# Hymba layer with 32 experts: fourteen expert blocks of up to 64 tokens run as 64-row blocks, high and low parts side by side, two of their eight gate/up slices as plain f32 products

## The reference, cut to what matters

```python
logits = xf @ w_router + b_router            # 512 tokens, 32 experts
top_v, top_e = lax.top_k(logits, 4)          # 4 experts per token: 2048 rows in all
gates = softmax(top_v)
# for every expert e, over the rows that chose it:
gu = xe @ w_gate_up[e] + b_gate_up[e]        # 1024 -> 2048, gate and up interleaved
gate = minimum(gu[..., 0::2], 7);  up = clip(gu[..., 1::2], -7, 7)
act = (up + 1.0) * (gate * sigmoid(1.702 * gate))
y = act @ w_down[e] + b_down[e]              # 1024 -> 1024
out[row_tok] += y * gate_of_row
```

## Time and profile before

| | us |
|---|---|
| time, median of 3 runs (lowest to highest) | 1488.14 (1487.26 to 1488.17) |
| span of the profiled execution, first to last instruction | 1485.0 |
| PE busy | 1443.0 (97%) |
| DVE busy | 1304.8 (88%) |
| ACT busy | 1017.6 (69%) |

### The profile page before, as it was taken

How to read it: one execution, slowest core, us unless ns; L and a number is a source line. 1 busy time by engine, 2 the same in 40 slices (tenths; PEclk the granted TensorE clock), 3 DMA queues, 4 the chain that set the end, 5 groups by cost and what they waited for, 6 DMA issues and landing times.

```text
span 1485.0 us, 21394 instructions
## 1 busy us (share of the span) xinstructions
PE 1443.0 (97%) x7006; PEld 1173.1 (79%) x7006; DVE 1304.8 (88%) x1230; ACT 1017.6 (69%) x913; POOL 274.3 (18%) x282
## 2 busy tenths in 40 slices
PE   6999999899999999999999999999999999999996
PEld 6877866878888888888888888888888888888883
DVE  7358575899999999999999999999999999999998
ACT  6344345377777777777777777777777777777772
POOL 0000000033222222222222232222222222222210
PEclk9999999899999999999999999999999999999998
DMA  9411130499999999999999999999999999999994
GB/s 349 143 58 57 34 142 15 180 327 391 377 388 375 373 379 374 376 367 372 367 370 375 375 377 365 377 377 378 376 377 377 375 375 375 370 377 362 373 378 178
DMA packets 102334, 472.64 MB, mean 318 GB/s; under 512 B 16499, under 2 KB 16539, under 8 KB 68000
## 3 DMA queue, kind: packets, MB, share of 16 engines
q1 hardware_dynamic: 87632, 451.71, 78.0%
q0 software_dynamic: 14672, 20.53, 3.9%
HBM read 467.70 MB, written 22.02 MB: 330 GB/s over the span
## 4 chain that ended last, share of the span: by engine, by line
PE 92%; DVE 6%; DMA 1%; ACT 1%; issue 1%; SPq 0%; DVEq 0%
PE gu_bank L1321 18%; PE gu_bank L1322 18%; PE gu_bank L1323 18%; PE turn_bank L1321 8%; PE turn_bank L1323 8%; PE turn_bank L1322 8%; PE bank L1608 2%; PE bank L1615 2%; PE bank L1321 1%; PE bank L1323 1%; PE bank L1322 1%; PE gu_bank L1461 1%; PE gu_bank L1601 1%; DMA arena<-in_x_dram 1%; DVE w_lo L873 1%; PE turn_bank L1487 1%
## 5 line engine op out<-in xcount | busy, mean ns | idle before, releaser
L873 DVE TENSOR_TENSOR w_lo<-raw,w_hi 128x2048 fp32r<-128x2048 f32 x411 | 931.7, 2289 | 98.3 <-ACT w_hi L605 93.5
L605 ACT ACTIVATE w_hi<-raw 128x2048 fp32r<-128x2048 f32 x411 | 784.6, 1920 | 209.1 <-PE gu_bank L1323 176.0
L1321 PE MATMUL gu_bank<-w_hi,turned 128*128 128x512 f32 x1080 | 423.8, 392 | 1.2 <-ACT arena L795 1.1
L1323 PE MATMUL gu_bank<-w_hi,turned 128*128 128x512 f32 x1080 | 420.5, 389 | 0.0
L1322 PE MATMUL gu_bank<-w_lo,turned 128*128 128x512 f32 x1080 | 420.4, 389 | 0.0
L1321 PEld LDWEIGHTS gu_bank<-w_hi,turned 128*128 128x128 f32 x1080 | 202.8, 188 | 43.6 <-ACT arena L795 1.4
L1323 PEld LDWEIGHTS gu_bank<-w_hi,turned 128*128 128x128 f32 x1080 | 202.7, 188 | 42.3
L1322 PEld LDWEIGHTS gu_bank<-w_lo,turned 128*128 128x128 f32 x1080 | 202.9, 188 | 40.7
L1321 PE MATMUL turn_bank<-w_hi,turned 128*128 128x512 f32 (+1 forms) x544 | 213.4, 392 | 0.0
L1323 PE MATMUL turn_bank<-w_hi,turned 128*128 128x512 f32 (+1 forms) x544 | 210.4, 387 | 0.0
L1322 PE MATMUL turn_bank<-w_lo,turned 128*128 128x512 f32 (+1 forms) x544 | 210.3, 387 | 0.0
(11 more groups left out here) (297 smaller groups left out, 1352.3 us busy)
## 6 DMA issues: line engine op xcount, KB each, us to landing
raw<-in_w_gate_up_dram SPq DMA_DIRECT2D x264, 1024.0 KB, 8.1
raw<-in_w_down_dram SPq DMA_DIRECT2D x132, 1024.0 KB, 8.9
raw<-in_w_in_dram SPq DMA_DIRECT2D x10, 1024.0 KB, 6.8
raw<-in_w_out_dram SPq DMA_DIRECT2D x4, 1024.0 KB, 5.0
raw<-expert_rows SPq DMA_DIRECT2D x4, 1024.0 KB, 6.4
raw<-in_w_mem_kv_dram SPq DMA_DIRECT2D x2, 1024.0 KB, 12.1
arena<-in_x_dram SPq DMA_DIRECT2D x1, 2048.0 KB, 13.7
arena<-in_position_tables_dram SPq DMA_DIRECT2D x1, 2048.0 KB, 18.0
```

Of the source, the lines that this page charges most:

```text
L605: a.activation(home, raw_ap, ACT.Copy).then_inc(hi_ready, 1)
L873: v.tensor_tensor(home[1], raw_ap, home[0].bitcast(F32), ALU.subtract).then_inc(lo_ready, 1)
L1321: pe.matmul(bank, a[0], b[0], start=first, stop=False)
L1323: return pe.matmul(bank, a[1], b[0], start=False, stop=last)
```

## The change

The changed kernel has two kinds of block. Fourteen experts of at most 64 tokens each (of the experts 1 to 31, in their order) become the odd blocks 1, 3, ..., 27: *narrow* blocks. All other blocks are *wide*, as before. Steps 1 to 28 thus form 14 pairs; step `b` with odd `b` does the gate/up of a narrow block and the down of a wide one (called here a narrow step), the next does the gate/up of a wide and the down of a narrow block (a wide step).

- In a narrow block `hx` holds the high parts of 64 rows in columns 0 to 63 and their low parts in columns 64 to 127, and `ha` likewise. A product is two matmuls (`two`: both halves times `w_hi`, both times `w_lo`), eight a slice; output rows 64 to 127 then hold what the low parts gave and are added to rows 0 to 63 later, by matmuls with a shifted identity (`fold_gate_up`, 4 matmuls, after d0; `fold_down`, 2 matmuls, after k0 of the next step), each behind a copy of the bank by ACT (`low_of_gate_up`, 128 x 2048; `low_of_down`, 128 x 1024).
- Slices k1 and k5 of a narrow block are not split. SP loads them into one buffer, `spare`; PE multiplies them as f32, four matmuls of 128 x 512 (`gate_up_whole`). The slot of `raw` and the counts of `lo_ready` that they would have had are stepped over.
- The clamp of a narrow block waits for its fold (`gu_folded`), and works on 64 rows. The rows of a narrow block leave one step later (`y_out_folded`), and POOL's scatter is one step later for every block. The loads of `g_final` and the down biases move behind the pairs.
- The routing finds the narrow experts and numbers the blocks anew: three small DVE instructions go and some twenty come.

The core of the diff (declarations, tables and the other engines' calls left out):

```diff
+            def whole(e, j, b):
+
+                k = WHOLE[j]
+                sp.wait_ge(lo_ready, b * 12 + (7 + k))
+                sp.sem_inc(raw_in[(GU + k) % 6], 16)
+                sp.wait_ge(half_used, b * 12 + (9 + k))
+                sp.dma_start(spare.rearrange("p (e n) -> p e n", e=1),
+                             gu_dram[bass.ds(e, 1), :, k, :].rearrange("e p n -> p e n")).then_inc(whole_in[j], 16)
...
+            def narrow_step(b):
+
+                before, e = experts_of(b)
+                for k in range(GU):
+                    if k == WHOLE[1]:
+                        whole(e, 0, b)
+                    elif k != WHOLE[0]:
+                        gate_up(e, k, GU + k, b * 12 + (7 + k))
+                for j in range(DN):
+                    if j == 2:
+                        whole(e, 1, b)
+                    down(before, j, 2 * GU + j, b * 12 + (7 + GU + j))
+
+            with sp.Fori(0, NARROW) as n:
+                narrow_step(n * 2 + 1)
+                wide_step(n * 2 + 2)
+            with sp.Fori(LOOP_FROM - 1, loops + 1) as b:
+                wide_step(b)
...
+            def narrow_after_wide(b, folded):
+
+                hi_m(GU + 4, b, 2)
+                if folded is not None:
+                    y_out_folded(folded, column(b - 2), b * 16)
+                hi_m(GU + 6, b)
+                turn_act(0, b)
+                turn_act(1, b)
+                for i in range(7, 11):
+                    hi_m(GU + i, b)
+                low_of_gate_up(b + 1)
+                hi_m(GU + 11, b)
...
-            link(v.tensor_scalar(n_blk, count, float(P), 1.0, ALU.is_gt, ALU.add))
-            for j in (2, 3):
-                link(v.scalar_tensor_tensor(out=n_blk, in0=count, scalar=float(P * j), in1=n_blk,
-                                            op0=ALU.is_gt, op1=ALU.add))
+            link(v.scalar_tensor_tensor(out=few, in0=count, scalar=NARROW_ROWS + 0.5, in1=cst[:, C_NOT_FIRST:C_NOT_FIRST + E],
+                                        op0=ALU.is_lt, op1=ALU.mult))
+            link(v.tensor_tensor_scan(few_seen, ones[:, 0:E], few, 0.0, ALU.mult, ALU.add))
...
+            def wide_after_narrow(b, narrow_next):
+
+                for i in range(4, 7):
+                    lo_m(GU + i, b)
+                turn_act_narrow(0, b * 2)
+                turn_act_narrow(1, b * 2 + 1)
+                for i in range(7, 11):
+                    lo_m(GU + i, b)
+                clamp(b + 1)
+                lo_m(GU + 11, b)
+                for q in range(2):
+                    if narrow_next:
+                        turn_x_narrow(q, b * 2 + (3 + q))
+                    else:
+                        turn_x(q, b * 2 + (3 + q))
+                activate(b + 1, b)
+                lo_m(GU + 12, b, 2 if narrow_next else 1)
+                for i in range(14 if narrow_next else 13, 16):
+                    lo_m(GU + i, b)
...
+            def two(bank, a, b, first=False, last=False):
+
+                pe.matmul(bank, a, b[0], start=first, stop=False)
+                return pe.matmul(bank, a, b[1], start=False, stop=last)
...
+            def gate_up_whole(j, n):
+
+                k = WHOLE[j]
+                pe.wait_ge(whole_in[j], n * 16)
+                for c in range(4):
+                    ins = pe.matmul(psum[c], hx[:, k, :].bitcast(F32), spare[:, c * 512:(c + 1) * 512],
+                                    start=False, stop=False)
                 ins.then_inc(half_used, 1)
...
+            def narrow_after_wide(b, n, between=None):
+
+                pe.wait_ge(xlo_ready, b * 2 + 2)
+                for k in range(GU):
+                    if k in WHOLE:
+                        gate_up_whole(WHOLE.index(k), n)
+                    else:
+                        gate_up(k, GU + k, b, between=between if k == 0 else None, narrow=True)
+                    if k == 0 and between is None:
+                        fold_down(n - 1)
+                    if k == 2:
+                        turn_acts(b)
+                gu_bias(b, narrow=True)
+                pe.wait_ge(alo_ready, b * 2)
+                turn_rows(b * 16 + 16)
+                pe.wait_ge(y_free, b)
+                for j in range(DN):
+                    down(j, 2 * GU + j, b)
+                    if j == 0:
+                        fold_gate_up(n)
```

More of the change, by code:

```diff
@@ L212, in hymba_layer @@
         n_blk = small(E)
+        few_seen, narrow_index, narrow_rows = (small(E) for _ in range(3))
+        rows_i = small(E).bitcast(I32)
+        narrow_from = small(E)
+        blk_two = small(NT * TOPK)
+        exp_wide, few = F[:, 15144:15144 + MAX_BLOCKS], F[:, 15192:15192 + E]
         b_end = small(E)
@@ L251, in hymba_layer @@
         g_final = F[:, 11264:12288]
+        spare = F[:, 11264:13312]
         back = raw[:, 0:NT, :]
@@ L581, in _, with steps @@
             pool.wait_ge(bias_saved, 16)
[L582 to L586, removed]
+            pool.wait_ge(xtp_done, 2)
+            gather(slice(2, 3), 3)
+            bias_of_block(1)
+            def steps(first, end):
+                with pool.Fori(first, end) as b:
+                    pool.wait_ge(xtp_done, b + 1)
+                    gather(bass.ds(b + 1, 1), b * 2)
+                    bias_of_block(b)
+                    scatter(b - 2, b * 2 + 1)
+            steps(2, LOOP_FROM)
+            pool.wait_ge(half_used, (LOOP_FROM - 3) * 12 + (13 + WHOLE[1]))
+            pool.dma_start(g_final, final_norm_g.unsqueeze(0).to_broadcast([P, D])).then_inc(gf_in, 16)
+            for t in range(NT):
+                pool.dma_start(b_dn[t * E:(t + 1) * E, :], b_down[0]).then_inc(gf_in, 16)
+            steps(LOOP_FROM, loops)
             pool.wait_ge(xtp_done, loops + 1)
             bias_of_block(loops)
+            scatter(loops - 2, loops * 2)
             scatter(loops - 1, loops * 2 + 1)
@@ L787, in _ @@
                 hi_m(i)
[L788 to L791, removed]
+            hi_m(GU, halves=2)
+            turn_x_narrow(0, 2)
+            turn_x_narrow(1, 2)
             hi_m(GU + 2)
@@ L803, in _, with column, wide_after_wide @@
             loops = a.value_load(loops_i[0:1, :], min_val=E - 1, max_val=MAX_LOOPS)
-            with a.Fori(1, loops) as b:
-                for i in range(4, 7):
-                    hi_m(GU + i, b)
+            def column(b):
+                return slice(b, b + 1) if isinstance(b, int) else bass.ds(b, 1)
+            def wide_after_wide(b, folded=None):
+                hi_m(GU + 4, b)
+                if folded is not None:
+                    y_out_folded(folded, column(b - 2), b * 16)
+                hi_m(GU + 5, b)
+                hi_m(GU + 6, b)
                 turn_act(0, b)
@@ L1574, in half_in, with gate_up @@
                 return half % 4
-            def gate_up(k, i, b, rows=(hx, lx), between=None):
+            def gate_up(k, i, b, rows=(hx, lx), between=None, narrow=False):
                 slot = half_in(i, b)
@@ L1581, in gate_up @@
                         between()
-                    ins = three(psum[c], (rows[0][:, k, :], rows[1][:, k, :]), w_part(slot, c * 512, (c + 1) * 512),
-                                first=k == 0)
+                    w = w_part(slot, c * 512, (c + 1) * 512)
+                    if narrow:
+                        ins = two(psum[c], hx[:, k, :], w, first=k == 0)
+                    else:
+                        ins = three(psum[c], (rows[0][:, k, :], rows[1][:, k, :]), w, first=k == 0)
+                ins.then_inc(half_used, 1)
+            def gate_up_whole(j, n):
[4 more added lines that the diff above has]
+                                    start=False, stop=False)
                 ins.then_inc(half_used, 1)
@@ L1617, in turn_acts, with down @@
                 ins.then_inc(atp_done, 1)
-            def down(j, i, b, rows=(ha, la), bank=4):
+            def down(j, i, b, rows=(ha, la), bank=4, narrow=False):
                 slot = half_in(i, b)
@@ L1625, in down @@
                         at0 = kk * D + c * 512
-                        ins = three(psum[bank + c], (rows[0][:, k, :], rows[1][:, k, :]),
-                                    w_part(slot, at0, at0 + 512), first=k == 0, last=k == KT - 1)
+                        if narrow:
+                            ins = two(psum[bank + c], ha[:, k, :], w_part(slot, at0, at0 + 512), first=k == 0, last=k == KT - 1)
+                        else:
+                            ins = three(psum[bank + c], (rows[0][:, k, :], rows[1][:, k, :]),
+                                        w_part(slot, at0, at0 + 512), first=k == 0, last=k == KT - 1)
                 ins.then_inc(half_used, 1)
```

282 lines of the change are left out of this document (231 added, 51 removed).

## The result

The changed kernel takes 1528.7 us (median of 4 runs, 1528.4 to 1529.61) where the kernel before takes 1488.08 in the same comparison: the ratio is 1.0277 (95% interval 1.0263 to 1.0292), 40.6 us slower. The forecast was 1489, with a range of 1450 to 1526; the time lies outside it, on the side to which the text gave half of the chance, and close to the 1538 of the rival on TensorE's clock.

What follows compares the result with a forecast made beforehand. PE was taken to bound the kernel before; after the change, a circle of load order through SP, PE and DVE. 1488.1 - 3.4 (14 pairs) + 4.4 (added ahead and behind) = 1489 us, range 1450 to 1526.

Steps and rivals of the forecast that it cites:

- the rival on TensorE's clock: PE's clock falls in the wait at k5, the f32 slice takes twice as long: +3.5 us a pair, 1538 us; chance 0.12.
- The circle of loads: Load order through SP, PE and DVE makes a pair last 69.8 us against 70.04, so PE's saving becomes idle time.
- Leg C: From the start of the wide step to the next narrow step's split of k0: 33.0 us.
- Leg A: From DVE's split of a narrow step's k0 to the landing of k5, fifth load behind it: 16.0 us.
- k5's own condition: The load of k5 needs PE done with k1, about 6 us after the split of k0; claimed met by then.
- The f32 slice: An unsplit slice on PE, four f32 matmuls of 128 x 512: taken as 3.5 us, dearer than the 2.72 it replaces.
- leg B: From the landing of k5 to the start of the wide step: 20.8 us.
- The ends: Costs outside the pairs: 3.9 us of added routing instructions ahead, 0.5 for one more fold and copy behind; together +4.4.
- the holes in the clock's digits: Sign against the forecast: the profile's clock digits showing holes between 300 and 1280 us.
- The queue isn't empty at T: Rival, chance 0.15: at DVE's split of k0, the first load behind it takes 8.1 us, not 4.6; 1523 us.
- The unsplit slices land in time: Rival, chance 0.12: k5 is there when k4 ends, PE or the DMA engines bound the pair; 1443 us.
- the base case: k5 lands late in the narrow step, pair 68.6 to 71 us; chance 0.61, own range 1474 to 1506 us.

Runs made afterwards that it cites:

- fill_wait: Changed kernel with 14 matmuls of no use on PE ahead of the second unsplit slice (k5), inside its wait; 1502.73 us, ratio 1.0093.
- k5_fourth: Changed kernel with the load of k5 one place earlier, behind d0 and ahead of d1; 1460.86 us, ratio 0.9811.
- fill_half: Changed kernel with 6 matmuls of no use on PE ahead of the second unsplit slice (k5); 1504.11 us, ratio 1.0127.
- before_17: Kernel before the change with 17 more small linked DVE instructions in the routing; 1492.23 us, ratio 1.0025.
- k5_first: Changed kernel with the load of k5 issued behind k7 and ahead of d0 instead of behind d1; 1469.19 us, ratio 0.9863.
- k5_in_ring: Changed kernel with k5 loaded, still unsplit, into the ring slot it stepped over, behind k4 and ahead of k6; 1448.79 us, ratio 0.9738.
- all_split: Changed kernel with k1 and k5 split, loaded and multiplied like the other slices, 64-row blocks kept; 1438.03 us, ratio 0.9672.

## Why the prediction was wrong, point by point

**The circle of loads: right.** Its three legs, from T at 837.82, where PE's wait for the split of k0 ends: k5 starts at 854.70, the wide step at 876.89, and the next such wait ends at 909.93. That makes 16.9, 22.2 and 33.0, against 16.0, 20.8 and 33.0. Leg C, which rests on a chain of eight durations from the earlier trace rows, is right to 0.1 us. The waits that it names are there: 14 at k5, 4.6 us each (3.5 foretold); 1.47 at the first slice of the narrow step (1.6); none at k1.

**The step that failed: that the clock's fall is a small chance.** "The trace shows the low level only where PE had much longer breaks, so I leave it at its small chance" was wrong; it fell in every pair, at waits of 4.1 to 5.9 us. The trace of before had no wait of this kind in a loop, so it could not speak against the rival. The price was 1.4 to 1.7 us in ten pairs and 2.1 to 3.1 in the other four (slices against 3.14), 26 us in all by fill_wait, and not the 3.5 a pair of the rival, since only the first part of the slice ran slow. Without the fall the time is 1502.73 (fill_wait), within the range of the forecast. The rule of the Trainium skill that stood beside this rival ("TensorE: Matmul & The Clock Gate", section "HAM oscillation", a wait for a load between products that costs the clock every time) describes what happened; the trace of the changed kernel agrees with it 14 times in 14, though PE's work between two such waits is over 60 us here. For shorter waits it did not hold: in k5_fourth twelve waits of up to 3.5 us left the clock up.

**The terms that were mis-sized.** Leg A was counted 0.9 short, and the wait with it. Its first load landed 4.9 us after its issue (4.6 counted), and the four behind it took 11.8 us to k5's start (2.95 each, 2.81 counted). POOL's scatter goes out at 843.98 in the middle of it, and from 846 to 850 us the transfers ran at 366 GB/s, against 424 behind. That the scatter is the cause was read from the trace, and not tried. The prediction also had k5's own condition, PE's use of k1, met by the time it was needed; SP waited some 1.0 us a pair for it (13.3 us in 13 waits). With d0 and d1 still under way, what this wait costs is not known. The f32 slice was taken too dear: 3.0 to 3.1 us from its first matmul to the first of the next slice, not 3.5; leg B without the fall is 20.5 (fill_wait, fill_half), so 0.3 were counted too many. The sum closes: 69.8 + 0.9 - 0.3 + 1.7 = 72.1 us a pair, as measured. The ends were taken at +4.4 and came to 14.1: 5.5 ahead of the first expert matmul (3.9 foretold; before_17 gave 4.1 us of time), 1.6 for the low clock behind it, which the forecast had not, 5.3 in the first narrow step, in which a pair's wait and slow slice (5.9 and 6.2 us) are paid before anything is saved, and 1.7 at the end.

**The signs.** The waits came, at 4.6 us for the foretold 3 to 4. Two other signs misled. PE's busy time went down by 49.6 us and not by some 80; the slow slices have a part in that, since k5_first, which has none, is 64.9 below the kernel before. And the holes in the clock's digits that were to prove the forecast wrong are not on the page of the changed kernel: its 40 digits are those of before, 9 everywhere but in the eighth slice (the end of the routing) and the last, which have 8 in both. A slice of the page is 38 us long; one in which 1.7 are lost is still at 95% of the clock and shows as 9, so windows of a few us are needed to see such a fall.

**The rivals.** "The queue isn't empty at T" didn't come by its mechanism, the first load taking 8.1 us: k6 landed 4.9 us after its issue. Leg A, at 16.9, passed the 16.6 from which that rival was to decide all the same, for the reasons above. "The unsplit slices land in time" was made by experiment, at 1448.79 in k5_in_ring, against the 1443 that its DMA bound gave.

**The chances.** 0.50 for slower went to the right side, but the time named was 1489, since the base case had it; two losses of the same wait, idle time and a slower slice, were treated as rivals of each other and belonged into one sum.

## What to carry to other kernels

A load that leaves the ring of its neighbours must be checked for its place in the queue and for what must be over before it is issued: here one load two places too late cost 59.5 us (k5_first), more than the 50 that the 64-row blocks gave (all_split). A wait of TensorE of several us that comes back in each turn of a loop is to be priced with the clock behind it, and some work of no use inside the wait tells in one run how much of the loss that is. Before a slice is taken off the split engines at TensorE's expense, ask whether those engines bound anything.

## What the runs showed of the hardware

An f32 matmul of 128x512 in a run of four cost 0.76 to 0.79 us of PE's time (a slice of 3.03 to 3.14 us, two records each), while the four-record stretches of the earlier trace rows give 0.91. The wait for k5 brought the granted clock down in 14 of 14 cases at 4.1 to 5.9 us, in 2 of 14 in k5_fourth (those of 4.1 and 4.5 us, and none of up to 3.5), and once in fill_half, at 3.0 us behind 1.7 us of matmuls; with 3.5 us of matmuls put into it, in none. The fall ended within the slice: in the pair shown the granted clock was 0.65 from 854 to 858 us, 0.93 from 858 to 862 and 1.00 from 862 to 866. One core drew 395 to 398 GB/s over 900 us in 1 MiB loads with scatters and gathers beside them.
